# A two-layer hybrid backbone on one core: the expert stage's order on TensorE regrouped, and nine buffers for expert weights

## The chip, the core and the metric

The program runs on one core of a Trainium2 chip. The metric is the device time of one execution, in microseconds (us). The kernel before took 1310.83 us (median of 3 runs, 1310.83 to 1314.21).

A core has engines that run on their own and wait for each other by semaphores: TensorE (PE in the profile; PEld are its weight loads), VectorE (DVE), ScalarE (ACT), GpSimd (POOL) and SyncE (SP), which here issues nearly all DMAs. SBUF is the memory on the core, PSUM the banks that TensorE writes.

## The reference, cut to what matters

Two groups of 128 tokens (prompt and sample) go through two layers, D = 1024, with one set of weights. A layer is a token mixer and a mixture of experts:

```python
mod = silu(c) @ w_mod[l] + b_mod[l]                     # six vectors of 1024: shift, scale, gate, twice
y = token_mixing(x * (1 + scale1) + shift1, ...)        # one input projection, three branches, output projection
x = layer_norm(ALPHA * x + gate1 * y, g, b)
h = x * (1 + scale2) + shift2
gate = top2_of_4_inside_the_best_of_4_groups(h @ w_rg, h @ w_re)       # 16 weights a token, two of them not zero
hid = silu(h @ w_e1[e]) * (h @ w_e3[e])                 # for each of 16 experts: 1024 -> 512
y = sum over e of (hid * gate[e]) @ w_e2[e]             # 512 -> 1024
x = layer_norm(ALPHA * x + gate2 * y, g, b)
```

All weights are float32. An expert has three matrices of 2 MiB: "up 0" (w_e1), "up 1" (w_e3) and "down" (w_e2). The modulation is 12 matrices of 2 MiB a layer.

## The kernel before, in words

Both groups are computed together: 256 tokens. A layer has four stages on TensorE: 18 chunks of the input projection, three branch products, the output projection with the routing, and the experts. Work is written out by hand for each engine, and each engine runs its list in order; `l` is the layer.

**The projection.** A chunk of w_in (2 MiB) comes into one of three ring buffers; the rounds of the branches (`h_round`, `t_round`) stand between the quarters of the chunks at places that `plan` works out. Among the chunks, by `MODS_AFTER`, stand products with a modulation matrix (`mod_products`, L967), 12 in layer 0 and 3 in layer 1. These 2 MiB matrices go through the same ring. All modulation rows must be there at `TURN_AT`, where they are summed and stored; the two gate vectors are read back for the norms.

**The routing.** After the output projection TensorE turns x, makes the routing logits and ranks the tokens of each expert. In layer 0 two more modulation products of layer 1 stand there (`router_mod`, `ROUTER_MODS`), in layer 1 products that are thrown away (`hold_clock`).

**The experts.** The tokens of an expert, at most 64, are gathered by products with a choice matrix (`gather_split`, bfloat16 in three parts, 24 matmuls for half of the features), into `xgT`, for two experts at a time. `up(j, e, i)` is the product of up matrix j with expert e + i: 16 matmuls of shape 128 rows by 64 columns, two beside each other. `down` has the same shape. `hid` is turned by two transposes (128 by 128), the choice matrix too (`sel_turned`), and the result of `down`, weighted on VectorE and split into three bfloat16 parts by ScalarE and VectorE in turn, is spread back to the tokens (`spread_group`, 64 rows by 128 columns, adding up in PSUM). A loop runs over pairs of experts, written out in `pair`; the first and the last pair are apart.

**The loads.** Eight buffers hold expert weights: two for an even expert's up matrices (`ahead_slot`), one for its down matrix (`even_down`), the ring of three for odd experts, and two that are filled once, before the experts begin, with the last expert's up 1 and down (`last_up`, `last_down`). A buffer's next load is issued by SP when `slot_used` says that TensorE has read it (`used_e`), in the order of SP's list (`expert_slot`, `even_slot`, `even_down_slot`). The loads share one DMA queue. The first pair also splits the 256 tokens into three bfloat16 parts on VectorE and ScalarE (`split_tokens`, `middle`), which `gather_split` needs.

At the end of layer 0's experts three modulation matrices (`LAYER_MODS`) come into the freed buffers and their products (L967) stand before layer 1's first chunk.

## Time and profile before

| | us |
|---|---|
| median of 3 runs | 1310.83 |
| profiled execution | 1309.18 |
| its span in the trace | 1307.4 |
| PE busy | 1264.1 (97%) |
| DVE / ACT / POOL busy | 629.6 / 267.2 / 139.2 |
| experts, layer 0 (first up product to last spread) | 442.1 to 667.3 |
| experts, layer 1 | 1070.1 to 1294.6 |

The profiled execution's own time lies 1.8 us over its span. A busy PE counts modelled ends of matmuls, so 97% does not say that nothing is lost; what is lost is read from the starts. In a row of PE a float32 matmul of the program is counted twice, since it is two instructions. In a row of the timeline what stands in square brackets is the idle time before it and what ended it.

### The profile page before, as it was taken

The numbers are of one execution on the slowest core, as the hardware profiler recorded it, in microseconds if no ns is written. First come the engines' busy times: TensorE is split into PE (matmuls) and PEld (weight loads), VectorE is DVE, ScalarE is ACT, GpSimd is POOL, SyncE is SP. The second block draws the span as 40 slices with busy tenths as digits, with TensorE's granted clock in tenths as the row PEclk, the third lists the DMA queues.
The fourth block names the chain that finished last, engine by engine and source line by source line (L and its number), as shares of the span: only waits on it lengthen the run. The fifth ranks groups of instructions, "written<-read, shape, count | busy, mean of one in ns | idle before, by whom it ended". The sixth has DMA issues, their size and how long they took to land.

```text
span 1307.4 us, 18971 instructions
## 1 busy us (share of the span) xinstructions
PE 1264.1 (97%) x7484; PEld 775.6 (59%) x7484; DVE 629.6 (48%) x1217; ACT 267.2 (20%) x572; POOL 139.2 (11%) x115
## 2 busy tenths in 40 slices
PE   6999999999999999999999999999999999999995
PEld 3675577477744655555548656855884465555552
DVE  1225455476333764454452345556753366544444
ACT  0021221233301211111120212203430122111111
POOL 0003432022200000000000034301230000000000
PEclk9999999999999999999999999999999999999998
DMA  9954653756649999999993536254445599999991
GB/s 377 342 228 174 233 210 137 272 227 269 233 160 375 396 427 428 429 429 428 429 403 130 223 131 226 98 199 154 153 155 227 207 348 428 427 428 428 429 428 59
DMA packets 47096, 375.30 MB, mean 287 GB/s; under 512 B 15272, under 2 KB 19512, under 8 KB 23864
## 3 DMA queue, kind: packets, MB, share of 16 engines
q1 hardware_dynamic: 38544, 371.14, 70.5%
q10 hardware_dynamic: 8488, 3.29, 1.0%
q8 instruction: 43, 0.70, 0.2%
q14 instruction: 21, 0.17, 0.0%
HBM read 370.07 MB, written 4.33 MB: 286 GB/s over the span
## 4 chain that ended last, share of the span: by engine, by line
PE 86%; DMA 7%; DVE 5%; issue 1%; ACT 1%; DVEq 0%; SPq 0%; ACTq 0%
PE psum L1275 17%; PE psum L1419 13%; PE psum L1222 9%; PE psum L1269 9%; PE psum L1479 7%; PE psum L1300 6%; PE psum L1314 4%; DMA ring<-in_stream 4%; PE psum L967 3%; PE psum L1427 2%; PE psum L1389 2%; PE psum L1030 2%; PE psum L950 2%; DMA ch<-in_stream 1%; DMA tbuf<-in_stream 1%
## 5 line engine op out<-in xcount | busy, mean ns | idle before, releaser
L1275 PE MATMUL psum<-ring,hT 128*128 128x512 f32 x512 | 228.7, 594 | 1.2 <-DVE hT L1908 0.8
L1275 PEld LDWEIGHTS psum<-ring,hT 128*128 128x128 f32 x512 | 93.5, 190 | 103.4 <-issue 101.1
L1269 PE MATMUL psum<-hT,ring 128*128 128x256 f32 x608 | 136.7, 380 | 0.0
L1269 PEld LDWEIGHTS psum<-hT,ring 128*128 128x128 f32 x608 | 113.7, 190 | 17.8 <-issue 3.5
L1419 PE MATMUL psum<-ch,tbuf 128*64 128x256 f32 x1024 | 113.3, 379 | 0.0
L1419 PE MATMUL psum<-ring,tbuf 128*64 128x256 f32 x960 | 106.8, 379 | 2.2 <-DMA ring<-in_stream 2.2
L1419 PEld LDWEIGHTS psum<-ch,tbuf 128*64 128x64 f32 x1024 | 73.4, 137 | 42.9 <-issue 8.0
L1419 PEld LDWEIGHTS psum<-ring,tbuf 128*64 128x64 f32 x960 | 69.6, 137 | 43.5 <-issue 7.0
L1300 PE MATMUL psum<-ring,tbuf 128*128 128x512 f32 x192 | 82.7, 592 | 0.0
L2565 POOL TENSOR_SCALAR ldata<-ldata 128x512 f32<-128x512 f32 x24 | 50.6, 2108 | 221.0 <-ACT ldata L1728 221.0
L2370 DVE TENSOR_SCALAR tbuf<-psum,tbuf 128x512 f32<-128x512 f32 x32 | 24.0, 751 | 103.1 <-PE psum L1479 103.1
L1300 PEld LDWEIGHTS psum<-ring,tbuf 128*128 128x128 f32 x192 | 36.5, 190 | 45.1 <-issue 45.0
L1479 PE MATMUL psum<-ring,tbuf 128*64 128x512 f32 x256 | 58.5, 598 | 0.9 <-ACT tbuf L1814 0.9
L1314 PE MATMUL psum<-ring,hT 128*128 128x512 f32 x128 | 55.8, 594 | 1.4 <-ACT hT L1762 1.4
L2390 DVE RECIPROCAL tbuf<-tbuf 128x256 f32<-128x256 f32 x32 | 56.1, 1753 | 1.1
L402 POOL TENSOR_TENSOR hbuf<-hbuf 128x512 f32<-128x512 f32 x28 | 45.5, 1627 | 93.4 <-PE psum L1030 93.4
L1222 PE MATMUL psum<-hbuf 128*128 128x256 f32 x240 | 54.9, 381 | 0.1
L1479 PE MATMUL psum<-ch,tbuf 128*64 128x512 f32 x224 | 51.2, 598 | 0.2 <-DMA ch<-in_stream 0.2
L2180 DVE TENSOR_TENSOR ch<-psum,bias_ring 128x512 f32<-128x512 f32 x28 | 19.3, 691 | 63.6 <-PE psum L1275 63.6
L1824 ACT ACTIVATE hbuf<-tbuf 128x512 bf16<-128x512 f32 x30 | 18.9, 630 | 148.2 <-DVE tbuf L2370 148.2
L1222 PEld LDWEIGHTS psum<-hbuf 128*128 128x128 f32 x240 | 44.5, 190 | 7.0 <-issue 1.2
L1427 PE MATMUL psum<-hbuf,tbuf 64*128 64x512 bf16 x360 | 46.8, 379 | 0.0
(349 smaller groups left out, 1607.1 us busy)
## 6 DMA issues: line engine op xcount, KB each, us to landing
ring<-in_stream SPq DMA_DIRECT2D x104, 2048.0 KB, 11.2
ch<-in_stream SPq DMA_DIRECT2D x51, 2048.0 KB, 18.3
bias_ring<-in_b_in SPq DMA_DIRECT2D x26, 256.0 KB, 8.1
ring<-in_stream SPq DMA_DIRECT2D x6, 1024.0 KB, 16.2
ldata<-in_ldata SPq DMA_DIRECT2D x2, 2329.0 KB, 17.5
tbuf<-in_stream SPq DMA_DIRECT2D x2, 2048.0 KB, 14.3
hbuf<-in_ln SPq DMA_DIRECT2D x4, 1024.0 KB, 10.0
ldata<-in_stream SPq DMA_DIRECT2D x2, 2048.0 KB, 12.5
```

The lines of the kernel that those rows point to most:

```text
L402: return engine.tensor_tensor(v, v, other.unsqueeze(3).to_broadcast([P, 2, W // (2 * half), half]), ALU.mult)
L967: mm = pe.matmul(psum[MROWS * j:MROWS * (j + 1), b, :], scZ[:, k, ZC - 2 * m:ZC - 2 * m + MROWS], w[:, k, :], start=(start and k < 4), sto ...
L1222: mm = pe.matmul(psum[:, product_bank(c, p), 0:HALF], a_block(a)[:, k, :], b_block(l, c, b)[:, k, :], start=(k == 0 and not on_top), stop= ...
L1269: mm = pe.matmul(psum[:, b, part * G * P:(part + 1) * G * P], w[:, k, (2 * g + part) * P:(2 * g + part + 1) * P], hT[:, k, :], start=(k == ...
L1275: mm = pe.matmul(bank(PJ + g), hT[:, k, g * P:(g + 1) * P], w[:, k, :], start=(k == 0), stop=(k == KT - 1))
L1300: mm = pe.matmul(bank(BR_BANK[g] + hf), rows_k, w[:, k, hf * W:(hf + 1) * W], start=(k == 0), stop=(k == BT - 1))
L1314: mm = pe.matmul(bank(2 * hf + g), hT[:, k, g * P:(g + 1) * P], w[:, k, :], start=(k == 0), stop=(k == KT - 1))
L1419: mm = pe.matmul(psum[halves_of[hf], UP[j], 0:FE // 2], xgT[:, k, halves_of[i]], w_k[:, hf * (FE // 2):(hf + 1) * (FE // 2)], start=(k == ...
L1427: mm = pe.matmul(bank(Y_MOE[g][hf]), e_selT[i][g][halves_of[hf], :], e_parts[halves_of[hf], s, :], start=opens and s == 0, stop=False)
L1479: mm = pe.matmul(psum[halves_of[hf], OUT, :], ehidT[:, (k % 2) * P + (k // 2) * CAP:(k % 2) * P + (k // 2) * CAP + CAP], w_down[:, k, hf * ...
L2390: mlink(dve.reciprocal(esig, esig))
L2565: pool.tensor_scalar(sig, sig, 1.0, LN_MAX, ALU.add, ALU.min).then_inc(sig_plus, 1)
```

## The change: what it does

1. **Nine buffers.** `extra` (two halves) is a ninth buffer. The buffers that are filled once now hold expert 1's down and up 1 (`second_down`, `second_up`), and `extra` holds expert 1's up 0 first and expert 15's up 0 afterwards. The ring therefore starts with expert 3. SP issues half of `extra`, `second_down` and half of `second_up` (4 MiB) after the loads of the branch matrices; before, the last expert's 4 MiB stood behind the first experts' loads. The norm's and gates' vectors of the second sub-layer (2 MiB) now go where `second_down` lies, and are loaded after expert 1's down product.
2. **Modulations moved.** Layer 1's products with matrices 10 and 11 leave the projection (chunks 6 and 10) and stand in layer 1's routing in place of `hold_clock`. Their rows are summed by one more product, which waits for VectorE's `add_router_mods` and stands before the gather; ScalarE copies the sum out and stores it.
3. **TensorE's order in a pair.** Products of one tile shape stand together, and the spreads of both experts stand in one piece. VectorE's and ScalarE's lists are reordered to match. The turned `hid` and the second half of the gathered tokens get other places in PSUM.
4. The layer's data (`ldata`) is loaded in two pieces; the first 2 MiB come later, since the norm's vectors lie there.

The numbers of lines in this diff are those of the two files; "..." is what is left out.

```diff
-              dict(zip([2, 6, 10], [(1, m) for m in range(9, N_MOD)]))]
-ROUTER_MODS, LAYER_MODS = [4, 5], [6, 7, 8]
+              {2: (1, 9)}]
+ROUTER_MODS, LAYER_MODS = [[4, 5], [10, 11]], [6, 7, 8]
...
+        extra = [hbuf[:, 0:4 * W], spare[:, :, :].rearrange("p a n -> p (a n)")]
+        gathered_late = psum[:, 0:2, FE // 2:FE]
+        hid_out = psum[:, XG, 0:FE // 2]
...
-                        norm_and_gates(l, 0)
+                        norm(l, 0)
+                        gates(l, 0)
+                        sp.wait_ge(t_dve, l * NT + NT)
+                        second = l * SLOTS + FIRST_EXPERT_SLOT + 3
+                        sp.dma_start(extra[1], dram["stream"][second, :, SLOT // 2:]).then_inc(extra_loaded, 16)
+                        sp.dma_start(second_down, dram["stream"][second + 2]).then_inc(second_down_loaded, 16)
+                        sp.wait_ge(proj_read, proj(l, N_IN - 1, 1))
...
-                expert_slot(1, 0, used(l, FIRST_EXPERT[l] - 3))
-                expert_slot(1, 1, used(l, FIRST_EXPERT[l] - 2))
+                expert_slot(3, 0, used(l, FIRST_EXPERT[l] - 3))
+                expert_slot(3, 1, used(l, FIRST_EXPERT[l] - 2))
                 expert_slot(0, 2, used(l, FIRST_EXPERT[l] - 1))
...
                 def first_pass():
...
+                    even_slot(2, 0, used_e(l, 0, 0, 0))
+                    even_slot(2, 1, used_e(l, 0, 0, 1))
+                    expert_slot(3, 2, used_e(l, 0, 0, 2))
                     sp.wait_ge(h2_split, l * G + G)
+                    even_down_slot(2, used_e(l, 0, 0, 2))
+                    sp.wait_ge(slot_used, used_e(l, 0, 1, 0))
+                    for i, piece in enumerate(extra):
+                        sp.dma_start(piece, dram["stream"][l * SLOTS + FIRST_EXPERT_SLOT + 3 * (NE - 1), :, ...])
+                    sp.wait_ge(slot_used, used_e(l, 0, 1, 2))
+                    norm(l, 1)
+                    gates(l, 1)
...
+                    def next_pair(e, last=False):
+                        even_slot(e + 2, 0, used_e(l, e, 0, 0))
+                        even_slot(e + 2, 1, used_e(l, e, 0, 1))
+                        if not last:
+                            expert_slot(e + 3, 0, used_e(l, e, 1, 0))
+                        expert_slot(e + 3, 1, used_e(l, e, 1, 1))
+                        even_down_slot(e + 2, used_e(l, e, 0, 2))
+                        expert_slot(e + 3, 2, used_e(l, e, 1, 2))
...
+                if l + 1 == DEPTH:
+                    pe.wait_ge(h2_ready, l * 4 + 4)
+                    pe.wait_ge(rows_added, len(MOD_ADDS))
+                    pe.matmul(psum[0:MROWS, EX + 1, :], fold, rows[:, l, :], start=True, stop=True).then_inc(rows_summed, 1)
...
                 def pair(e, first=False, last=False):
...
+                    n = step(l, e)
+                    up(1, e, 0, ahead=True)
+                    pe.wait_ge(moe_chain, n * 3 + 3)
+                    up(0, e, 1, first=first, last=last)
+                    turn_hidden(n)
+                    turn_choice(n)
+                    up(1, e, 1, first=first)
+                    down(n, e, 0, first, last)
+                    if not last:
+                        gather_split(n + 2, 0, first=first)
+                        pe.wait_ge(hid_ready, n + 2)
+                        gather_split(n + 2, 1)
+                        pe.wait_ge(xg_ready, n + 3)
+                    turn_hidden(n + 1)
+                    turn_choice(n + 1)
+                    if not first:
+                        spread_rows(n - 1, 1)
+                    if last:
+                        down(n + 1, e, 1, first, last)
+                        spread_rows(n, 0)
...
+                    else:
+                        spread_rows(n, 0, opens=first)
+                        pe.wait_ge(xg_ready, n + 4)
+                        pe.wait_ge(hidT_ready, n + 2)
+                        up(0, e + 2, 0, ahead=True)
+                        down(n + 1, e, 1, first, last)
```

TensorE, the loop over pairs (layer 0), before. L1419 is `up` (32 matmuls are two of them), L1479 `down`, L1389 a half of the gather, L1447 the turned choice, L1458 the turned `hid`, L1427 the spreads (6 are half an expert's).

```order
L1447 MATMUL psum<-tbuf 128x132 x2
L1427 MATMUL psum<-hbuf,tbuf 128x512 x6
L1458 MATMUL psum<-const,tbuf 128x128 x2
L1427 MATMUL psum<-hbuf,tbuf 128x512 x6
L1479 MATMUL psum<-ch,tbuf 64x512 x8
...
L1419 MATMUL psum<-ring,tbuf 64x256 x32
...
L1389 MATMUL psum<-tbuf,hbuf 128x128 x24
L1447 MATMUL psum<-tbuf 128x132 x2
L1427 MATMUL psum<-hbuf,tbuf 128x512 x12
L1458 MATMUL psum<-const,tbuf 128x128 x2
...
L1389 MATMUL psum<-tbuf,hbuf 128x128 x24
...
L1479 MATMUL psum<-ring,tbuf 64x512 x8
```

The same loop now. L1438 is `up`, L1495 `down`, L1401 the gather, L1468 the turned choice, L1460 the turned `hid`, L1446 the spreads.

```order
L1438 MATMUL psum<-ring,tbuf 64x256 x16
...
L1460 MATMUL psum<-const,tbuf 128x128 x2
L1468 MATMUL psum<-tbuf 128x132 x2
...
L1438 MATMUL psum<-ring,tbuf 64x256 x16
L1495 MATMUL psum<-ch,tbuf 64x512 x8
...
L1401 MATMUL psum<-tbuf,hbuf 128x128 x48
...
L1460 MATMUL psum<-const,tbuf 128x128 x2
L1468 MATMUL psum<-tbuf 128x132 x2
L1446 MATMUL psum<-hbuf,tbuf 128x512 x24
...
L1438 MATMUL psum<-ch,tbuf 64x256 x16
...
L1495 MATMUL psum<-ring,tbuf 64x512 x8
```

The number of matmuls of a pair is the same; the shape changed nine times in a round of the loop before and changes five times now.

SP, from the second sub-layer's first expert loads to the loop (layer 0), before: `ch` is `ahead_slot` and `even_down`, `ldata`, `hT`, `values` and `bias_ring` hold the last expert, `hbuf` and `spare` the norm's and gates' vectors.

```order
L853 DMA ring<-in_stream 128x4096 x3
L865 DMA ldata<-in_stream 128x4096
L871 DMA hT<-in_stream 128x2048
L871 DMA values<-in_stream 128x1024
L871 DMA bias_ring<-in_stream 128x1024
L759 DMA hbuf<-in_ln 128x2048
L761 DMA spare<-row_mem 128x2048
L858 DMA ch<-in_stream 128x4096 x2
L853 DMA ring<-in_stream 128x4096 x3
L880 DMA ch<-in_stream 128x4096
L853 DMA ring<-in_stream 128x4096
```

The same place now: the ring holds expert 0's down and expert 3, and `hbuf` with `spare` is the ninth buffer.

```order
L872 DMA ring<-in_stream 128x4096 x3
L883 DMA hbuf<-in_stream 128x2048
L885 DMA hT<-in_stream 128x2048
L877 DMA ch<-in_stream 128x4096 x2
L872 DMA ring<-in_stream 128x4096
L890 DMA ch<-in_stream 128x4096
L900 DMA hbuf<-in_stream 128x2048
L900 DMA spare<-in_stream 128x2048
L764 DMA ldata<-in_ln 128x2048
L770 DMA ldata<-row_mem 128x2048
```

The last expert's 4 MiB are gone from the front, one ring load stands between the first even loads and the even down matrix, where three stood, and the vectors stand last, behind expert 1's down product.

VectorE, the first pair, before: L2341 and L2344 split the tokens, L2389 to L2391 are the silu of expert 1, L2366 and L2370 weight expert 0's rows, L2384 takes gathered tokens in.

```order
L2351 TENSOR_SCALAR tbuf<-const,tbuf 128x64 x4
L2341 TENSOR_TENSOR hbuf<-ch,hbuf 128x1024
L2344 TENSOR_TENSOR hbuf<-hbuf 128x1024
L2341 TENSOR_TENSOR hbuf<-ch,hbuf 128x1024
L2344 TENSOR_TENSOR hbuf<-hbuf 128x1024
L2366 TENSOR_REDUCE tbuf<-tbuf 128x1
L2370 TENSOR_SCALAR tbuf<-psum,tbuf 128x512
L2376 TENSOR_TENSOR tbuf<-tbuf,hbuf 128x512
L2379 TENSOR_TENSOR hbuf<-tbuf,hbuf 128x512
L2389 TENSOR_SCALAR tbuf<-tbuf 128x256
L2390 RECIPROCAL tbuf<-tbuf 128x256
L2391 TENSOR_TENSOR tbuf<-tbuf,psum 128x256
```

The same place now: L2396 and L2399 split, L2449 to L2451 are the silu, L2457 makes expert 1's `hid`, L2421 and L2426 weight expert 0's rows, L2444 takes tokens in.

```order
L2396 TENSOR_TENSOR hbuf<-ch,hbuf 128x1024
L2399 TENSOR_TENSOR hbuf<-hbuf 128x1024
L2449 TENSOR_SCALAR tbuf<-tbuf 128x256
L2450 RECIPROCAL tbuf<-tbuf 128x256
L2451 TENSOR_TENSOR tbuf<-tbuf,psum 128x256
...
L2457 TENSOR_TENSOR tbuf<-tbuf,psum 128x256
L2421 TENSOR_REDUCE tbuf<-tbuf 128x1
L2426 TENSOR_SCALAR tbuf<-psum,tbuf 128x512
L2444 COPY tbuf<-psum 128x512
L2431 TENSOR_TENSOR tbuf<-tbuf,hbuf 128x512
L2444 COPY tbuf<-psum 128x512
L2437 TENSOR_TENSOR hbuf<-tbuf,hbuf 128x512
```

Expert 1's silu and `hid` now stand between the split of the tokens and the weighting of expert 0's rows, and the two copies of gathered tokens stand inside the split of the rows.

## Rows read from the trace of the kernel before

**Rows 1.** The page's first part: busy us, share of the span, instructions.

```profile
PE 1264.1 (97%) x7484; PEld 775.6 (59%) x7484; DVE 629.6 (48%) x1217; ACT 267.2 (20%) x572; POOL 139.2 (11%) x115
```

**Rows 2.** Stretches: length, busy of each engine, clock granted, DMA share, GB/s.

```profile
438.40:442.10 3.70, 3.70 (x32) 3.60 (x32) 1.01 (x2) 0.33 (x1) 0.00 (x0) 1.00 0.98 363
442.10:667.30 225.20, 220.82 (x1873) 123.16 (x1873) 112.46 (x242) 39.40 (x80) 0.00 (x0) 1.00 1.01 427
...
672.70:1056.00 383.30, 381.14 (x1642) 250.86 (x1642) 184.15 (x317) 87.53 (x193) 69.26 (x56) 1.00 0.50 184
1064.80:1070.06 5.26, 5.26 (x32) 5.14 (x32) 0.69 (x1) 0.34 (x1) 0.00 (x0) 0.69 1.00 356
1070.06:1294.60 224.54, 220.76 (x1869) 121.96 (x1868) 112.77 (x242) 39.39 (x80) 0.00 (x0) 1.00 0.92 390
```

**Rows 3.** PE in order of time, a pair: start, length, line, tiles, shape, count.

```profile
522.81 3.65 PE L1479 MATMUL psum<-ring,tbuf 128*64 128x512 f32 x16
...
534.27 0.44 PE L1458 MATMUL psum<-const,tbuf 128*128 128x128 f32 x2
534.64 0.82 PE L1427 MATMUL psum<-hbuf,tbuf 64*128 64x512 bf16 x6
...
538.88 7.08 PE L1419 MATMUL psum<-ring,tbuf 128*64 128x256 f32 x64
545.89 1.51 PE L1389 MATMUL psum<-tbuf,hbuf 128*128 128x128 bf16 x24
547.24 0.28 PE L1447 MATMUL psum<-tbuf 128*128 128x132 bf16 x2
...
548.85 0.44 PE L1458 MATMUL psum<-const,tbuf 128*128 128x128 f32 x2
549.12 1.50 PE L1389 MATMUL psum<-tbuf,hbuf 128*128 128x128 bf16 x24
550.55 0.65 PE L1479 MATMUL psum<-ring,tbuf 128*64 128x512 f32 x2
```

**Rows 4.** PE in order of time, expert 13's up 0.

```profile
626.92 3.67 PE L1419 MATMUL psum<-ring,tbuf 128*64 128x256 f32 x32 [1.18 <-DMA ring<-in_stream]
```

**Rows 5.** Ring loads, issue to landing: issued at 946.2; seven, issued 570.5 to 625.8.

```profile
DMA to landing us min/median/max: 7.6/7.6/7.6
...
DMA to landing us min/median/max: 20.3/23.6/25.6
```

**Rows 6.** SP in order of time: expert 2's up matrices, layer 0.

```profile
445.84 3.78 SPq L858 DMA_DIRECT2D ch<-in_stream  x2
```

**Rows 7.** DVE in order of time, the first pair of layer 0.

```profile
448.99 0.42 DVE L2391 TENSOR_TENSOR tbuf<-tbuf,psum 128x256 f32<-128x256 f32 x1
...
450.90 1.22 DVE L2341 TENSOR_TENSOR hbuf<-ch,hbuf 128x1024 f32<-128x1024 f32 x1
453.31 1.23 DVE L2344 TENSOR_TENSOR hbuf<-hbuf 128x1024 bf16<-128x1024 f32 x1 [1.19 <-ACT hbuf L1798]
...
458.39 0.75 DVE L2370 TENSOR_SCALAR tbuf<-psum,tbuf 128x512 f32<-128x512 f32 x1
459.83 0.69 DVE L2376 TENSOR_TENSOR tbuf<-tbuf,hbuf 128x512 f32<-128x512 f32 x1 [0.70 <-ACT hbuf L1824]
```

**Rows 8.** PE in order of time: from layer 0's experts to layer 1.

```profile
667.27 5.36 PE L967 MATMUL psum<-ch,scZ 128*32 128x512 f32 x48
```

**Rows 9.** PE in order of time, layer 1, the modulation product after chunk 6.

```profile
788.23 1.92 PE L967 MATMUL psum<-ring,scZ 128*32 128x512 f32 x16
790.09 1.09 PE L950 MATMUL psum<-const,hbuf 128*128 128x128 f32 x8
```

**Rows 10.** In order of time: a sum of rows, the router's add, layer 1's gather.

```profile
335.76 1.05 PE L1249 MATMUL psum<-rows,const 128*32 128x512 f32 x2
...
438.04 0.68 DVE L2335 TENSOR_TENSOR rows<-rows,psum 128x512 f32<-128x512 f32 x1
...
1064.79 5.34 PE L1399 MATMUL psum<-tbuf,ch 128*128 128x128 f32 x32 [0.90 <-DVE tbuf L2351]
```

More of the change, by code:

```diff
@@ new lines, in turn_hidden, with turn_choice @@
+                def turn_hidden(n):
+                    pe.wait_ge(hid_ready, n + 1)
+                    for j in range(2):
+                        mm = pe.transpose(hid_out[:, j * P:(j + 1) * P], ehid[:, j * P:(j + 1) * P], ident)
+                    mm.then_inc(hid_turned, 1)
+                def turn_choice(n):
+                    pe.wait_ge(sel_ready, n + 1)
+                    pe.wait_ge(out_read, n)
+                    for g in (1, 0):
+                        mm = pe.matmul(psum[:, OUT, (1 - g) * (P + 4):(2 - g) * (P + 4)], e_sel[:, g, :], around_ident[:, 4 * g:4 * g + P + 4],
+                                       start=True, stop=True)
+                    mm.then_inc(sel_turned, 1)
@@ new lines, in spread_rows, with down @@
+                def spread_rows(n, i, opens=False):
+                    pe.wait_ge(selT_ready, n + 1)
+                    pe.wait_ge(eout_ready, n + 1)
+                    for g in range(G):
+                        spread_group(i, g, opens)
+                def down(n, e, i, first, last):
+                    pe.wait_ge(hidT_ready, n + 1)
+                    pe.wait_ge(selT_ready, n + 1)
+                    from_even = i == 0 and not first
+                    if from_even:
+                        pe.wait_ge(even_down_loaded, e * 8 + l * ((NE // 2 - 1) * 16))
+                    elif i == 0:
+                        pe.wait_ge(slot_loaded[ring_e(l, 2)], first_down_arrived(l))
+                    elif first:
+                        pe.wait_ge(second_down_loaded, l * 16 + 16)
+                    else:
+                        pe.wait_ge(slot_loaded[ring_e(l, 2)], arrived_e(l, e + i, 2))
+                    w_down = w_down_even if from_even else w_down_second if i == 1 and first else w_down_ring
+                    for k in range(BT):
+                        for hf in range(2):
+                            mm = pe.matmul(psum[halves_of[hf], OUT, :], ehidT[:, (k % 2) * P + (k // 2) * CAP:(k % 2) * P + (k // 2) * CAP + CAP],
+                                           w_down[:, k, hf * W:(hf + 1) * W], start=(k == 0), stop=(k == BT - 1))
+                    mm.then_inc(slot_used, 1)
@@ new lines, in pair @@
+                def pair(e, first=False, last=False):
+                    n = step(l, e)
+                    sigmoid_exp(n + 1, e, 1)
+                    hidden(n)
+                    choice(n, turned_slots[0], first)
+                    if first:
+                        middle(0)
+                        middle(1)
+                    split_rows(n, 0)
+                    hidden(n + 1)
+                    choice(n + 1, turned_last if last else turned_slots[1], first)
+                    if last:
+                        act.wait_ge(eout_ready, n + 1)
+                        act.sem_inc(out_high, 1)
+                        act.sem_inc(out_middle, 1)
+                    else:
+                        sigmoid_exp(n + 2, e + 2, 0)
+                        if first and l + 1 == DEPTH:
+                            act.wait_ge(rows_stored, (l + 2) * 16)
+                        split_rows(n + 1, 1)
@@ new lines, in pair @@
+                    n = step(l, e)
+                    hidden(n, e, 0)
+                    if not last:
+                        pick_pair(n + 2, e + 2, e_pick_b)
+                    if first:
+                        for g in range(G):
+                            split_tokens(g)
+                    silu(n + 1)
+                    select(n + 1, e + 1)
+                    hidden(n + 1, e, 1)
+                    weighted_rows(n, e, 0, turned_slots[0], first)
+                    if not last:
+                        tokens_in(n + 2, 0, XG)
@@ new lines, in pair @@
+                    left_of_high(n, 0)
+                    if not last:
+                        tokens_in(n + 3, 1, None)
+                    left_of_middle(n, 0)
+                    if not last:
+                        select(n + 2, e + 2)
+                        if first:
+                            for g in range(G):
+                                link(ts(x[:, g, :], x[:, g, :], ALPHA, None, ALU.mult))
+                        silu(n + 2)
+                        weighted_rows(n + 1, e, 1, turned_slots[1], first)
+                        left_of_high(n + 1, 1)
+                        left_of_middle(n + 1, 1)
+                    else:
+                        weighted_rows(n + 1, e, 1, turned_last)
+                        dve.sem_inc(out_left, 1)
+                        dve.sem_inc(eout_ready, 1)
```

329 lines of the change are left out of this document (121 added, 208 removed).

## The prediction

> **What bounds the kernel now.** I read the page's first part, then the stretches, then TensorE's order of time in the experts, then the loads. The first says that TensorE is busy for 97% of the span [rows 1], so a gain must take work or waits from it. The stretches say that the two expert stages take 225.2 and 224.5 us and that in layer 0's the DMA queue has no free time at all, 427 GB/s with a share of 1.01 [rows 2]. Both are near their limit there, so I looked at which is nearer. A pair of experts takes 550.55 - 522.81 = 27.74 us on TensorE [rows 3]. A matrix of 2 MiB (2.097 MB) takes 2.097 / 427 = 4.91 us, and a pair needs six: 29.5 us. The loads thus lose 1.7 us a pair against TensorE, and only the lead from before the first pair pays for it. One sees that in the loads: a lone one lands 7.6 us after its issue, near the end of the stage they take 20.3 to 25.6 us [rows 5], and at 626.92 TensorE waits 1.18 us for one [rows 4]. So before, the loads catch up with TensorE just as the stage ends. Whatever makes TensorE faster here is worth something only if the loads come earlier too.
>
> **TensorE's order.** The matmuls of a pair stay. What goes is four of nine changes of shape. Their price: a turn of hid followed by another product of its shape takes 549.12 - 548.85 = 0.27 us, followed by a spread 534.64 - 534.27 = 0.37; half a gather takes 547.24 - 545.89 = 1.35 before its own shape and 550.55 - 549.12 = 1.43 before the other [rows 3]. So 0.1 us each, 0.4 us a pair, and a pair becomes 27.3 us. Two up products take 545.89 - 538.88 = 7.01 us with the change behind them, so 3.43 us for one alone.
>
> The Trainium skill (TensorEngine Tiling (Array Packing), section Key Properties) says that changing the tiling mode drains TensorE, where changing only the tile does not. The trace agrees in direction, with the 0.1 us above. By that rule alone fewer changes are a gain in every pair; what that would come to is the first rival below.
>
> **The loads of the expert stage, layer 0.** The first pair decides, so I carry it with rows of before.
> - Expert 0's silu ends on VectorE at 448.99 + 0.42 = 449.41 [rows 7]. TensorE now needs it for expert 1's up 0, 0.5 us after the second up product (442.1 + 2 x 3.43 = 449.0). Then up 0 (3.43), turns with two changes (0.65), up 1 and down (6.87): expert 0's down ends at 460.4.
> - Expert 2's up matrices are issued as before, at 445.84 and 3.45 us later [rows 6], but the queue is empty by then: the preload ends at about 443.5 (worked out: half of the ninth buffer and of expert 1's up 1, 1 MiB each at 2.45 us, issued when layer 0's routing products are done, about 435.8, with 7.6 - 4.9 = 2.7 us ahead of the first). They land at 458.5. The next load waits for expert 0's down: issued 460.7, flowing from 463.5. So the queue stands empty for some 5 us twice, and some 5 us before the preload's last part. These 15 us eat up what the 4 MiB that now come in the branch stage (2 x 4.91 = 9.8 us) would have gained, and more.
> - The three loads then last to 463.5 + 3 x 4.91 = 478.2. Behind them come the norm's and gates' vectors (4.9 us together), which wait for expert 1's down. When does that end? VectorE now splits the tokens (1.22, a wait of 1.19 for ScalarE, 1.23, twice [rows 7]) before expert 1's silu (2.5 us). ScalarE starts its part only after TensorE's turns, about 454.4, so the split ends at 460.3, silu and hid at 463.75, and TensorE waits 1.9 us before the second half of the gather (that half overwrites a bank which hid is read from). Weighting, copy, split of the rows, 0.75 and 0.69 each with 0.70 for ScalarE [rows 7], make the spread ready at 467.6: another 2.0 us of waits. Up and down (6.87) end at 475.9; the vectors flow from 478.9, 0.7 us after the queue ran dry, to 483.8.
> - From there the queue is full: 29 matrices to expert 12's down, 483.8 + 29 x 4.91 = 626.2. TensorE's own pace would bring it there at 475.9 + 5 x 27.3 + 11.2 = 623.6, so it waits 2.6 us in all and the shorter pairs are swallowed.
> - Rest of the stage by TensorE: down 3.43, gather and turns 3.3, spreads 2.7, a wait of 0.35 for expert 14's up 0, then 30.2 us (up, down, two ups, turns, up and down, turns, spread 1.4, down 3.7, spread 1.3, last spread 1.9). It ends at 666.2, against 667.27 [rows 8].
> - Layer 1's three modulation matrices are the next in the queue; the last lands at 626.2 + 9 x 4.91 = 670.4. Its product began at 667.27 + 2 x 5.36 / 3 = 670.85 before [rows 8]. Gain at the start of layer 1: **0.4 us** (bounds 1.2 and a loss of 1).
>
> The Trainium skill (DMA: Bandwidth & Descriptors, section Where 436 GB/s comes from) says that for HBM to SBUF the HBM side binds at about 358 GB/s. By that a matrix would take 5.86 us, and 33 of them 31 us more in each layer than I count. The trace disagrees: 427 GB/s over 225 us [rows 2]. I keep 427.
>
> **The moved modulations.** A product with its change of shape costs 790.09 - 788.23 = 1.86 us [rows 9], and two leave layer 1's projection. TensorE is busy there 381.14 of 383.30 us [rows 2], so nothing else is late when they go: **3.7 us** (bounds 0, if a branch round is late instead, and 3.7). Their loads leave as well, hidden before. In the routing they stand in for products that are thrown away, as in layer 0: nothing (bounds -0.5 and 0.5), since their 4 MiB start at about 1021 less the gain, more than 25 us ahead. What layer 1 gets anew is the sum of rows: the gather waits for the router's add, which ended at 438.04 + 0.68 = 438.7 in layer 0, 0.3 us after the gather began at 438.4 [rows 2, 10], plus some 0.3 to be seen by TensorE, and for the sum itself, 1.05 us [rows 10]. In place of 1064.79 the gather begins 1.6 us later. Before, TensorE's clock fell to its lower level there, 1.2 GHz (granted 0.69 in the mean over 5.26 us, against 3.70 us of the same work in layer 0) after waits of which 0.90 us is the last [rows 2, 10]. With the sum inside, the gap before it grows, so I let the clock fall as before: **1.6 us lost** (bounds 0, if the clock stays, as in layer 0, and 3.2, if it falls twice).
>
> **The expert stage, layer 1.** The same course as in layer 0, 666.2 - 442.1 = 224.1 us, against 224.54 [rows 2]: **0.45 us** (bounds 2.5, PE's pace alone, and a loss of 3). ScalarE's late copy of the sum and the store have the length of a pair to hide in. The final norms stay.
>
> **The sum.** 0.4 + 3.7 - 1.6 + 0.45 = 2.95 us less. The profiled execution took 1309.18 (its span is 1307.4); it becomes 1306.2. The median of the runs is 1.65 above it: 1310.83 - 2.95 = **1307.9**, 0.22% less. What a measurement of this kernel can tell from no change is about 0.3%, 3.9 us, so the likeliest outcome lies just within it.
>
> **Rivals.**
> - *TensorE sets the end of both expert stages* (by what the page on tiling says, fewer drains are a gain). For it: TensorE waits for loads just once, 1.18 us [rows 4]. Against: the queue's rate has no reserve. Six pairs by 0.4, that wait, the weighting at the end (about 0.9, now beside a spread), less 2.6 in the first pair (4.4 us of waits against about 1.8): 1.9 to 2.3 a layer, so 2.1 x 2 in place of 0.85: 1304.6. If the first pair's waits don't come either, 1300.
> - *The clock falls in the first pair* (slower). TensorE stands still twice there, 1.9 and 2.0 us, longer than the 0.90 us before the fall in layer 1. One fall costs 5.26 - 3.70 = 1.56 us [rows 2] and delays expert 1's down, hence the vectors, hence the full queue, by as much; two a layer cost 6.2: 1314.1. From one fall a layer on the change is no longer faster. Against it: in layer 0 the waits before the gather brought no fall.
> - *The projection doesn't get shorter*, since a round of the branches takes the place of the products: 1307.9 + 3.7 = 1311.6. Against: the 2 us of waits in 383.
>
> **Chances.** The forecast 0.53, its own range 1304.5 to 1311; TensorE sets the end 0.18; clock 0.15; projection 0.09; something else 0.05, mostly slower. Below 1306.9 lie a bit over 0.4 of the forecast and nearly all of the first rival: 0.40. Above 1314.8 lie half of the clock rival and what else is slower: 0.12. Within: 0.48. Range 1301.5 to 1315.
>
> **What would show it.** Right: in the expert stages of after, loads 4.9 us apart without a gap from about 464 to 670, gaps of some 5 us twice between 443 and 464, waits of TensorE for DMA from expert 10 on, 2 to 3 us in all; pairs of 27.3 us in the middle and over 29 at the end; waits of 1.5 to 2 us at the gather's second half and before the first spread; two modulation products fewer. Wrong: pairs of 27.3 us to the end, or a granted clock of 0.5 in the first pair, or a wait of some 2 us where the products were.

## The result, and the profile after

The changed kernel takes 1313.79 us (median of 20 runs, 1310.87 to 1318.03) against 1310.82 before (20 runs): a ratio of 1.0021, 95% interval 1.0013 to 1.0030. It is slower by about 2.8 us, where 2.9 us faster was forecast; the time lies inside the range. The profiled execution took 1313.28, its span is 1311.5. Where its 4.1 us went is read from the stretches (columns as in [rows 2]): layer 0's experts to the end of the last spread, layer 1's projection, its routing from the ranking to the first up product, its experts; the last row is the middle of layer 0's experts.

```profile
443.39:670.57 227.18, 218.36 (x1870) 124.16 (x1869) 112.56 (x242) 36.75 (x80) 0.00 (x0) 1.00 0.97 407
675.97:1055.35 379.38, 377.21 (x1622) 249.88 (x1622) 182.79 (x315) 87.58 (x193) 68.88 (x56) 1.00 0.53 201
1061.89:1070.90 9.01, 7.63 (x44) 6.60 (x44) 2.65 (x11) 2.91 (x4) 0.00 (x0) 0.81 0.66 242
1070.90:1298.75 227.85, 219.72 (x1869) 124.00 (x1868) 112.36 (x242) 36.75 (x80) 0.00 (x0) 0.99 0.90 378
480.00:629.00 149.00, 145.50 (x1276) 84.17 (x1271) 71.55 (x154) 23.63 (x54) 0.00 (x0) 1.00 1.01 428
```

| stretch | before | after | forecast | measured |
|---|---|---|---|---|
| experts, layer 0, with the boundary | 225.17 | 227.18 | -0.4 | +2.0 |
| projection, layer 1 | 383.46 | 379.38 | -3.7 | -4.1 |
| routing, layer 1 | 7.45 | 9.01 | +1.6 | +1.6 |
| experts, layer 1 | 224.55 | 227.85 | -0.45 | +3.3 |

They sum to 2.8 us. (That the medians differ by 2.8 us too is in part chance: these are two executions, each somewhere among the runs of its kernel.) The other 1.3 us is the start. TensorE's second modulation product took 3.30 us in place of 1.92, first the kernel before, then the changed one; in the trace's records the clock came to its upper level at 13.30 us and at 18.04:

```profile
15.33 1.92 PE L967 MATMUL psum<-tbuf,scZ 128*32 128x512 f32 x16 [1.93 <-DMA tbuf<-in_stream]
...
15.21 3.30 PE L981 MATMUL psum<-tbuf,scZ 128*32 128x512 f32 x16 [2.12 <-DMA tbuf<-in_stream]
```

The first ranking of layer 0 began anywhere from 436.1 to 440.1 in the kernels below, and in the kernel before at 436.20 in one trace and at about 437.6 in that of e4, which starts with the same list. So I do not put that to the change; all the stage times below leave it out.

TensorE in layer 0's first pair (columns as in [rows 3]), then a pair from the middle by its first and last up product:

```profile
450.74 1.95 PE L1438 MATMUL psum<-hbuf,tbuf 128*64 128x256 f32 x16 [0.22 <-DVE tbuf L2451]
...
461.86 1.51 PE L1401 MATMUL psum<-tbuf,hbuf 128*128 128x128 bf16 x24
464.92 1.51 PE L1401 MATMUL psum<-tbuf,hbuf 128*128 128x128 bf16 x24 [1.54 <-DVE tbuf L2457]
...
468.71 1.47 PE L1446 MATMUL psum<-hbuf,tbuf 64*128 64x512 bf16 x12 [1.79 <-DVE hbuf L2437]
...
504.36 3.62 PE L1438 MATMUL psum<-ch,tbuf 128*64 128x256 f32 x32
...
531.68 3.62 PE L1438 MATMUL psum<-ch,tbuf 128*64 128x256 f32 x32
```

The forecast waits of the first pair are there (0.22, 1.54 and 1.79 for 0.5, 1.9 and 2.0), and a pair takes 531.68 - 504.36 = 27.32 us for 27.74 [rows 3]. In the last pair there are two waits that the forecast does not have; ScalarE's rows (ACT) stand among TensorE's:

```profile
656.70 3.60 PE L1495 MATMUL psum<-ch,tbuf 128*64 128x512 f32 x16
660.23 0.44 PE L1460 MATMUL psum<-const,tbuf 128*128 128x128 f32 x2
...
661.19 0.63 ACT L1857 ACTIVATE hbuf<-tbuf 128x512 bf16<-128x512 f32 x1 [7.34 <-DVE tbuf L2426]
661.31 0.28 PE L1468 MATMUL psum<-tbuf 128*128 128x132 bf16 x2 [0.64 <-DVE tbuf L2426]
661.51 1.47 PE L1446 MATMUL psum<-hbuf,tbuf 64*128 64x512 bf16 x12
...
662.58 0.63 ACT L1859 ACTIVATE hbuf<-tbuf 128x512 bf16<-128x512 f32 x1 [0.76 <-DVE tbuf L2431]
663.12 0.37 ACT L1845 ACTIVATE tbuf<-psum 128x256 f32<-128x256 f32 x1
...
663.86 3.65 PE L1495 MATMUL psum<-ring,tbuf 128*64 128x512 f32 x16 [0.88 <-ACT tbuf L1845]
```

The first wait, 0.64 us, is for VectorE. The turned choice is written over what expert 14's down product left, so VectorE's weighting of those rows (L2426) has to read that first; in the other pairs the gather stands between the two and covers it, in the last pair there is no gather. The second, 0.88 us, comes of ScalarE's order. Expert 15's turned hid is there at 660.7, but ScalarE copies it (L1845) only at 663.12, behind its two parts of expert 14's split (L1857, L1859). Nothing is left for TensorE in that time: the spreads that stood between these steps before now stand in one piece.

The queue's gaps in the first pair:

```profile
443.70:448.30 4.60, 4.60 (x46) 3.08 (x44) 3.94 (x23) 0.38 (x1) 0.00 (x0) 1.00 0.23 48
458.50:462.60 4.10, 4.10 (x29) 1.60 (x26) 2.87 (x4) 1.06 (x1) 0.00 (x0) 1.00 0.04 16
478.50:480.00 1.50, 1.50 (x18) 1.00 (x14) 0.69 (x1) 0.74 (x2) 0.00 (x0) 1.00 0.76 208
```

The loads on both sides of the last of them, by their issue (start, length of the issuing) and their time from issue to landing:

```profile
463.29 0.69 SPq L900 DMA_DIRECT2D spare<-in_stream  x1
477.63 0.43 SPq L770 DMA_DIRECT2D ldata<-row_mem  x1
...
spare<-in_stream SPq DMA_DIRECT2D x1, 1024.0 KB, 16.9
ldata<-row_mem SPq DMA_DIRECT2D x1, 1024.0 KB, 9.4
```

TensorE's waits for loads in layer 0's experts (total us, times, longest), two rows of the kernel before and then three of the changed one:

```profile
PE psum L1419 <- DMA ring<-in_stream: 1.2, 1, 1.2
PE psum L1479 <- DMA ch<-in_stream: 0.2, 1, 0.2
...
PE psum L1495 <- DMA ch<-in_stream: 2.8, 3, 1.3
...
PE psum L1438 <- DMA ch<-in_stream: 0.6, 3, 0.2
PE psum L1438 <- DMA ring<-in_stream: 0.4, 2, 0.2
```

The queue stands nearly empty for 4.6 and 4.1 us, moves half its rate (208 GB/s) for 1.5 us, and from then on it is full (428 GB/s). TensorE waits 3.8 us for loads, against 1.4 us before.

Last, the clock in layer 1's first pair:

```profile
1096.65:1100.06 3.41, 3.41 (x18) 1.50 (x16) 1.19 (x2) 0.00 (x0) 0.00 (x0) 0.50 1.03 442
```

It is the lower level, 1.2 GHz, right behind the two waits. Layer 0's first pair kept the upper one in this execution.

### The profile page after: what moved, and what is told of

Read it like the earlier page. It is cut to its first block, busy times and chain, and to the rows that moved or that the text cites. A ratio compares the mean times of both kernels' runs of the same rounds, so it can differ in the third digit from the quotient of the medians.

```text
span 1311.5 us, 19020 instructions
## 1 busy us (share of the span) xinstructions
PE 1259.3 (96%) x7478; PEld 777.8 (59%) x7478; DVE 628.2 (48%) x1216; ACT 262.6 (20%) x573; POOL 138.8 (11%) x115
## 4 chain that ended last, share of the span: by engine, by line
PE 82%; DMA 9%; DVE 6%; issue 2%; ACT 1%; SPq 0%; ACTq 0%; DVEq 0%
PE psum L1291 17%; PE psum L1438 12%; PE psum L1236 9%; PE psum L1285 9%; DMA ch<-in_stream 8%; PE psum L1316 6%; PE psum L1495 6%; PE psum L1330 4%; PE psum L981 3%; PE psum L1044 2%; PE psum L1446 2%; PE psum L964 2%; PE psum L1401 1%; DMA tbuf<-in_stream 1%; PE psum L1412 1%
## 5 line engine op out<-in xcount | busy, mean ns | idle before, releaser
L1438 PE MATMUL psum<-ch,tbuf 128*64 128x256 f32 x1024 | 117.1, 382 | 1.2 <-DMA ch<-in_stream 1.2
L1438 PEld LDWEIGHTS psum<-ch,tbuf 128*64 128x64 f32 x1024 | 72.4, 138 | 49.2 <-issue 12.4
L1438 PE MATMUL psum<-ring,tbuf 128*64 128x256 f32 x832 | 94.9, 381 | 0.5 <-DMA ring<-in_stream 0.5
L1438 PEld LDWEIGHTS psum<-ring,tbuf 128*64 128x64 f32 x832 | 58.4, 137 | 30.3 <-DMA ring<-in_stream 1.1
L2449 DVE TENSOR_SCALAR tbuf<-tbuf 128x256 f32<-128x256 f32 x32 | 9.4, 293 | 111.8 <-ACT tbuf L1840 111.8
L1495 PE MATMUL psum<-ring,tbuf 128*64 128x512 f32 x256 | 57.7, 593 | 1.8 <-ACT tbuf L1845 1.8
L1495 PE MATMUL psum<-ch,tbuf 128*64 128x512 f32 x224 | 50.7, 594 | 5.1 <-DMA ch<-in_stream 5.1
L1857 ACT ACTIVATE hbuf<-tbuf 128x512 bf16<-128x512 f32 x30 | 18.9, 630 | 176.0 <-DVE tbuf L2426 176.0
L2426 DVE TENSOR_SCALAR tbuf<-psum,tbuf 128x512 f32<-128x512 f32 x32 | 24.0, 751 | 60.6 <-PE psum L1495 47.5
```

Source lines behind the costliest of these rows:

```text
L1438: mm = pe.matmul(psum[halves_of[hf], UP[j], 0:FE // 2], xgT[:, k, halves_of[i]], w_up[k][:, hf * (FE // 2):(hf + 1) * (FE // 2)], start=(k ...
L1495: mm = pe.matmul(psum[halves_of[hf], OUT, :], ehidT[:, (k % 2) * P + (k // 2) * CAP:(k % 2) * P + (k // 2) * CAP + CAP], w_down[:, k, hf * ...
```

## The experiments

Each is timed against runs of the kernel before on its own chip; the ratio is to those. Kernels whose stages take the same time differ by up to 0.0018 in it, some 2.4 us (the changed kernel 1.0021, e6 1.0003), so the argument goes by the stages; there, two traces of one and the same list differ by up to some 0.55 us (e5 below). Stage times run from the first up product to the begin of the last spread, in the changed kernel and those built on it with the spread's weight load: 223.23 us in layer 0 and 222.56 in layer 1 before, 225.15 and 225.75 in the changed kernel. The 225.75 holds the fall of the clock; e1, e2, e5 and e7 have none there, so what they gain in layer 0 is the cleaner figure. "Layer 1's way" is from that last spread of layer 0 to layer 1's ranking: 397.25 before, 393.35 after.

**e1: the tokens' split earlier.** ScalarE's list in the first pair:

```diff
+                    if first:
+                        middle(0); middle(1)
                     sigmoid_exp(n + 1, e, 1)
                     hidden(n)
                     choice(n, turned_slots[0], first)
-                    if first:
-                        middle(0); middle(1)
```

> Theory (the loads bind the stage, and the first pair's waits delay them): ScalarE makes its part of the token split before the exponential of expert 1, so VectorE's split ends about 3 us earlier; the waits of 1.54 us before the gather's second half and 1.79 us before the first spread shrink to under 0.8 together in each layer. Expert 1's down product ends some 2.7 us earlier, the norm's and gates' vectors are issued 2.7 us earlier and every later load lands 2.7 us earlier. TensorE's waits for loads stay near 1.7 us a layer, each expert stage gets 2.7 us shorter, and the clock does not fall in layer 1's first pair (another 1.6 us): the median falls by 5 to 7 us, to 1307 to 1309. Rival (the first pair's waits are hidden, since the loads are late anyway): the waits for loads grow by what the first pair gains, and the time changes by less than 1.5 us.

Measured: 1309.75, ratio 0.9990 (0.9979 to 1.0002).

```profile
442.01:666.24 224.23, 216.23 (x1859) 123.39 (x1860) 112.01 (x241) 36.67 (x80) 0.00 (x0) 1.00 0.97 407
...
1059.58:1066.96 7.38, 6.00 (x44) 4.98 (x44) 2.64 (x11) 2.92 (x4) 0.00 (x0) 1.00 0.78 295
1066.96:1291.42 224.46, 216.30 (x1859) 122.77 (x1860) 111.73 (x241) 36.66 (x80) 0.00 (x0) 1.00 0.91 383
```

```profile
PE psum L1495 <- DMA ch<-in_stream: 3.9, 3, 1.3
PE psum L1446 <- DVE hbuf L2437: 1.2, 1, 1.2
```

The first pair's waits fell from 3.3 to 1.2 us, but layer 0's stage only by 0.9, since the waits for loads grew by 1.1. In layer 0's stage the rival was right on the size. By the ratios the whole kernel gained 4.1 us over the changed one, more than the rival allowed: the clock stayed up in layer 1, in the routing too, which is 1.6 us shorter and which neither expected.

**e2: the vectors last.** `norm(l, 1)` and `gates(l, 1)` move behind `next_pair(NE - 4, last=True)` in SP's list.

> The norm's and gates' vectors (2 MiB) are loaded behind the last expert's matrices, not between expert 1's down and expert 4. Theory (the queue binds): all loads from expert 4's up to expert 15's land 4.9 us earlier, TensorE's waits for loads (1.7 us a layer) vanish; layer 0 gains 1.3 us only, since the three modulation matrices at its end still land at the same time (the last at 673), layer 1 gains 1.6: about -3 us, 1311. Rival (buffers that come free late set the landings, not the queue): landings and waits stay as they are, within 0.5 us. Rival 2: the norm now waits for its vectors, and the time grows by 2 us or more.

Measured: 1312.27, ratio 1.0015 (0.9998 to 1.0032). Layer 0's last products:

```profile
663.57 1.88 PE L1452 MATMUL psum<-tbuf 64*128 64x512 f32 x8
665.38 1.92 PE L980 MATMUL psum<-ch,scZ 128*32 128x512 f32 x16
669.06 1.92 PE L980 MATMUL psum<-ch,scZ 128*32 128x512 f32 x16 [1.76 <-DMA ch<-in_stream]
673.98 1.92 PE L980 MATMUL psum<-ch,scZ 128*32 128x512 f32 x16 [2.99 <-DMA ch<-in_stream]
```

The stages became 221.19 and 221.33, 4.0 and 4.4 us shorter, and layer 0's waits for loads went from 3.8 to 0.5 us: they were the queue's, twice what I had expected (I had counted only the 1.7 us around expert 12's down, and those around expert 10's cost as much). In layer 0 it comes back as 1.76 + 2.99 us in front of layer 1's modulations, which end the same queue. By the ratios the time is only 0.8 us under the changed kernel's, where the theory had 3. The profiled execution, 1308.45, was the fastest of the twelve and has no fall of the clock in a first pair; the mean granted clock of the twelve, 0.9918, is the lowest of all kernels here. So the clock is the likely reason, but no run shows it.

**e3: the modulations back.** The table has `{2, 6, 10}` again, the routing of layer 1 its `hold_clock`, and no sum of rows stands before the gather.

> The two modulation products go back into layer 1's projection, and the routing of layer 1 gets its thrown-away products back; the rest is as in the changed kernel. Theory: the projection costs 4.0 us more, the routing 1.6 us less, so +2.4 us, 1316.2; if the fall of the clock in layer 1's first pair goes with the sum of rows, +0.9. Rival (the moved modulations are what made the kernel slower, by the sum of rows and the clock): the time falls by 1.5 us or more. Rival 2: moving them was worth nothing, within 1 us.

Measured: 1317.21, ratio 1.0046 (1.0028 to 1.0064), by the ratios 3.3 us over the changed kernel. Layer 1's way is 397.76 (4.4 more), the routing 7.56 (1.5 less). So the move is worth some 2.9 us, and it is not what made the kernel slower.

**e4: the kernel before, with the vectors last.** The same edit in before.py's list, asking what loads cost there.

> The kernel before, with the norm's and gates' vectors loaded behind the last expert's matrices. It asks what the loads cost there. Theory (before, the loads catch up only at the very end): all loads of the experts land 2.0 us earlier, the one wait for a load goes, so layer 0's experts take 1.2 us less and layer 1's 1.0 less, while the modulations behind layer 0 come 2.9 us later and their last product waits 0.6: -1.6 us in all. Rival (the loads bind that kernel as they bind the changed one): 3 to 4 us less in each expert stage.

Measured: 1309.75, ratio 0.9983 (0.9972 to 0.9995). Stages 222.46 and 222.33: 0.8 and 0.2 less, where the changed kernel gave 4.0 and 4.4. But the edit did not free that kernel of its loads. It brought them only some 0.8 us earlier by the stage's own time, and a wait of 0.7 us stayed where 1.2 had been:

```profile
627.51 3.67 PE L1419 MATMUL psum<-ring,tbuf 128*64 128x256 f32 x32 [0.66 <-DMA ring<-in_stream]
```

So the run bears out little; that the loads cost little before is read from their waits, 1.4 us in all.

**e5: the last pair.**

```diff
                     turn_hidden(n + 1)
+                    if last:
+                        spread_rows(n - 1, 1)
                     turn_choice(n + 1)
...                  # ScalarE, last pair: hidden(n + 1), choice(n + 1), then split_rows(n, 0)
```

> In the last pair the spread of expert 13 goes ahead of the turned choice, and ScalarE copies expert 15's turned hid and choice before it splits expert 14's rows. Theory: the waits of 0.64 and 0.88 us in the last pair of each layer shrink to about 0.5 together, 1.0 us a layer, -2 us, 1311.8; layer 0's gain is real only as long as the modulation matrices at its end land in time (the last at 673, needed at 673.1 then). Rival (the waits only move): the spread of expert 14 waits instead for its rows, and the time changes by less than 0.5 us.

Measured: 1311.13, ratio 1.0002 (0.9989 to 1.0016), and

```profile
656.10 3.60 PE L1495 MATMUL psum<-ch,tbuf 128*64 128x512 f32 x16
...
660.00 1.47 PE L1446 MATMUL psum<-hbuf,tbuf 64*128 64x512 bf16 x12
661.40 0.29 PE L1468 MATMUL psum<-tbuf 128*128 128x132 bf16 x2
662.22 3.65 PE L1495 MATMUL psum<-ring,tbuf 128*64 128x512 f32 x16 [0.53 <-issue]
```

Stages 223.55 and 224.22, 1.6 and 1.5 us shorter. Not all of that is the edit. From expert 14's down to expert 15's it is 662.22 - 656.10 = 6.12 us here and 663.86 - 656.70 = 7.16 in the changed kernel: about 1.05 of the 1.52 us came back, and 0.53 stays as the time that the turned hid takes to come back from ScalarE. What the edit took out came back whole, since it stands behind the last load that is waited for. The other 0.55 us of layer 0 lies ahead of the last pair, where both lists are the same and the loads landed earlier in this trace; in layer 1 the fall of the clock is missing.

**e6: expert 15's up 0 first.** SP issues the two halves of `extra` right behind expert 2's up matrices.

> Expert 15's up 0 is issued ahead of the loads that wait for expert 0's down (as soon as expert 1's up 0 is read), so it fills the queue where it stood empty for some 4 us. Theory (the queue is filled, but the vectors behind expert 1's down set its next start): the loads of the first pair land 4.3 us earlier, the queue then runs dry until the vectors come as before, and everything from the vectors on lands where it did; the time stays within 0.7 us of the changed kernel's 1313.8. Rival (every load moves up by what is filled): all landings 4.3 us earlier, the waits for loads (3.8 us in layer 0's experts) go, 2 to 4 us less a layer, 1306 to 1310.

Measured: 1312.25, ratio 1.0003 (0.9990 to 1.0016). The queue, filled and then dry:

```profile
463.00:474.00 11.00, 7.66 (x68) 4.47 (x67) 7.01 (x17) 1.81 (x4) 0.00 (x0) 0.84 0.98 390
474.00:480.50 6.50, 6.50 (x48) 3.13 (x46) 3.41 (x6) 1.01 (x2) 0.00 (x0) 1.00 0.19 63
```

The gap moved by one place, as the theory had it: the vectors wait for expert 1's down. Stages 225.67 and 225.73, no shorter. The granted 0.84 of the first row holds a fall of the clock behind the first pair's second wait, in layer 0 this time; layer 1 has one too, as in the changed kernel, so there the two are like for like. By the ratio the kernel is 2.4 us under the changed one, which no stage shows.

**e7: both (e6 and e1).**

> The last edit and the earlier split together. Theory (the two gate each other): the vectors are issued some 2 us earlier, as with the earlier split alone, and now find the queue empty, so the loads from expert 4 on land 2 to 3 us earlier in their stage than in the changed kernel (1.0 with the split alone), each expert stage gets 2 to 3 us shorter than the changed kernel's 225.15 and 225.75 (0.9 and 1.3 with the split alone), and the mean granted clock stays at the 0.995 of the split alone: 1305 to 1308. Rival (what the split alone gave is all there is): stages of 224.2 and 224.5, 1309.7.

Measured: 1307.36, ratio 0.9971 (0.9960 to 0.9983). Stages 222.24 and 222.22, 2.9 and 3.5 us shorter, where e1 alone gave 0.9 and 1.3 and e6 nothing. Each removes the wait that hid the other. (Layer 1's figures hold the missing fall as well.)

**e8: all five.** e1, e2, e5, e6, and in layer 1 `add_router_mods` stands ahead of VectorE's wait for the ranks.

> The five edits together: earlier split, expert 15's up 0 first, vectors last, the last pair's order, and layer 1's rows added before the ranks come, so that their sum stands in the wait before the gather. Theory: no load is waited for in the experts (4.0 us a layer gained with the vectors last), the last pair gives 1.0 to 1.6, the split 2.9, less what TensorE's own pace then bounds: expert stages of 217 to 220 us against 225.15 and 225.75, no lateness of layer 1's modulations (393.3 from the last spread to layer 1's ranking, not 398), layer 1's route 7.6 in place of 9.0: 1296 to 1301. Rival (the loads of layer 0 still end at the same time, and the modulations wait): layer 0 gains nothing, 1302 to 1306.

Measured: 1303.68, ratio 0.9939 (0.9920 to 0.9958). Stages 218.50 and 218.25, the routing 6.01 for 9.01; but layer 1's way is 399.95, 6.6 us longer, with 2.43 and 2.98 us of waits before the modulations and a fall of the clock right behind them:

```profile
669.05 1.92 PE L980 MATMUL psum<-ch,scZ 128*32 128x512 f32 x16 [2.43 <-DMA ch<-in_stream]
673.95 2.67 PE L980 MATMUL psum<-ch,scZ 128*32 128x512 f32 x16 [2.98 <-DMA ch<-in_stream]
```

The rival took back layer 0's gain.

**e10: products that are thrown away in the waits.** `hold_clock(1, bank(2))` before `pe.wait_ge(hid_ready, n + 2)` and before the first spread.

> The changed kernel with two products that are thrown away, one in each wait of the first pair (before the gather's second half and before the first spread). Theory (the falls of the clock that the changed kernel shows more often come from TensorE standing still there): stages as in the changed kernel within 0.3 us where the clock holds, mean granted clock over the runs 0.995 in place of 0.993, the median 1.5 us less, 1312.3. Rival (the falls have nothing to do with these waits): clock 0.993, 1313.8.

Measured: 1311.74, ratio 1.0006 (0.9994 to 1.0018), mean granted clock 0.9943, standard error 0.0006, from 0.9932 with 0.0006. Its trace has no fall in either first pair, and 0.64 and 0.88 us of the waits are left; but the difference in the mean is not clear, and the trace, the slowest execution of the twelve (1317.46), has a fall in layer 0's gather ahead of the first pair. Open by this run.

**e11: the five, the vectors in layer 0 behind expert 4's first up matrix.**

> The five edits, but in layer 0 the vectors go behind expert 4's first up matrix, where the queue still stood empty for 3.1 us, and stay last in layer 1. Theory (layer 0 ends by the queue): the experts' loads land 1.8 us later than with the five edits, the modulations 3.1 us earlier; layer 0's experts 219 to 220.5 us in place of 218.5, from the last spread to layer 1's ranking 394 to 396 in place of 399.95: 1299.5 to 1301.5. Rival (the later loads cost TensorE as much as the modulations gain): 1303 to 1304.

Measured: 1298.24 (6 executions, as e12), ratio 0.9899 (0.9882 to 0.9917), faster than both kernels and 1.3 us below the low end of what was expected.

```profile
443.42:663.57 220.15, 215.83 (x1860) 123.35 (x1861) 112.06 (x241) 36.79 (x80) 0.00 (x0) 1.00 0.98 414
663.57:1056.90 393.33, 390.78 (x1732) 256.60 (x1728) 192.23 (x341) 91.91 (x203) 68.88 (x56) 1.00 0.54 204
1056.90:1062.92 6.02, 6.02 (x45) 4.98 (x45) 2.61 (x11) 2.91 (x4) 0.00 (x0) 1.00 0.89 329
1062.92:1281.21 218.29, 215.47 (x1860) 123.03 (x1861) 111.87 (x241) 36.78 (x80) 0.00 (x0) 1.00 0.95 395
```

**e12: the five, the vectors last in layer 1 alone.**

> The five edits, but in layer 0 the vectors stay where the changed kernel has them, behind expert 1's down, and go last in layer 1 alone. Theory: layer 0's experts take the 222.24 us of the two edits together less 1.5 for the last pair, 220.7, and the modulations are in time, 393.4; layer 1 as with the five edits: 1299.5 to 1301.5. Rival: as with the five edits, 1303.7, since what the experts lose the modulations gain.

Measured: 1299.09, ratio 0.9905 (0.9887 to 0.9922). Stages 221.17 and 218.21, layer 1's way 393.35. Layer 0 is 0.5 us over the forecast.

**e13: e1 in layer 1 alone.**

> The changed kernel with the earlier split in layer 1 alone. It asks whether the falls of the clock belong to the first pair's waits of their own layer. Theory (a fall comes from TensorE standing still shortly before it): layer 0 and layer 1's routing as in the changed kernel (stage 225.15 us, route 9.0 with a fall to the lower level), no fall in layer 1's first pair, layer 1's stage 224.5; mean granted clock over the runs 0.994, between the 0.9927 of the kernels with both layers' waits and the 0.9952 of those without; 1312 to 1313. Rival (the fall in layer 1's routing goes wherever the split is early, by chance of the traces taken so far or by something later in the program): route 7.4 without a fall, clock 0.995, 1310 to 1311.

Measured: 1312.25, ratio 1.0004 (0.9992 to 1.0016), mean clock 0.9936 (standard error 0.0005). Layer 0's first pair shows a fall right behind its waits, layer 1's none:

```profile
471.25:474.66 3.41, 3.41 (x18) 1.55 (x16) 0.94 (x2) 0.00 (x0) 0.00 (x0) 0.50 1.05 447
```

That is what the theory said of the first pairs. It fails on the routing: 7.39 us without a fall, though nothing ahead of it was changed and its wait of 1.38 us for the rows stayed:

```profile
1066.93 1.02 PE L1384 MATMUL psum<-rows,const 128*32 128x512 f32 x2 [1.38 <-DVE rows L2393]
```

## Why the prediction was wrong

Its direction was wrong by two terms of the expert stages; the rest of the sum held. The times of after are 1.27 us late by the start; that is taken off in this section.

- **TensorE's order: right.** 27.32 us a pair for 27.3. The gain of 0.42 us a pair is there and, as forecast, does not reach the end, since the loads set the pace. The Trainium skill (TensorEngine Tiling (Array Packing), section Key Properties) has the drain at a change of tiling mode; the trace agrees, at 0.1 us each.
- **The first pair: right.** Expert 0's down ended at 460.6 for 460.4, expert 1's at 475.8 for 475.9. e1, e6 and e7 show the chain as the text had it: split, expert 1's down, vectors, full queue.
- **The vectors' load: too small.** "the vectors flow from 478.9, 0.7 us after the queue ran dry, to 483.8": they landed at 485.7. The load ahead of them (`spare`) landed at 463.29 + 16.9 - 1.27 = 478.9 for 478.2, and they took another 6.8 us (to 477.63 + 9.4 - 1.27) where 5.6 were forecast. Both stand right behind an empty place of the queue, in the second case at half its rate (208 GB/s). With 29 matrices behind them, 4.9 us each as forecast, expert 12's down began at 627.8 for 626.2. That is 1.6 us of each layer. Why the queue comes up late is not shown.
- **The step that failed: "Rest of the stage by TensorE".** It gave the last pair 30.2 us and a wait of 0.35 us, 40.0 from expert 12's down to the end; it took 670.57 - 629.05 = 41.5. I added up TensorE's products and did not walk the lists of the engines that answer: with no gather there, the turned choice waits for VectorE's weighting (0.64), and with the spreads in one piece, expert 15's turned hid is queued behind ScalarE's two halves of a split (0.88). That is 1.5 us a layer, and a better order takes out 1.05 of it (e5).
- **The boundary: wrong.** I held that the modulations' loads end at 670.4 and hide TensorE's end at 666.2. TensorE ended at 669.3, and they were in time: the last landed at 671.7, later than forecast too, but its product began only at 672.9. What it costs when TensorE is earlier shows in e2, 1.76 + 2.99 us.
- **The modulations and the routing: right**, 4.1 for 3.7 (the stretch) and 1.6 for 1.6; e3 has 4.4 and 1.5. The "some 0.3" us that the router's add was to take until TensorE sees it was a guess without a row; here the sum begins 0.15 us after the add ends (1064.56 and 1064.41).
- **Layer 1: the same two terms**, 1.6 + 1.5, and a fall of the clock. The two give 224.1 + 3.1 = 227.2; measured 227.85, and the 0.65 left over is about what a fall costs (below).

The rivals. *TensorE sets the end* is refuted: 3.8 us of waits for loads, and 4.0 us less where they come earlier (e2). *The clock falls in the first pair* was real in part. Every fall in a first pair (five, in the traces of the changed kernel, e3, e6 and e13) stood right behind the two waits. Over all executions the mean granted clock was 0.9927 (62 executions, standard error 0.0003) in the kernels with both waits in both layers (the changed one, e2, e3, e5, e6) and 0.9952 (41, 0.0003) in those where the early split left one wait of 1.2 us (e1, e7, e8, e11, e12). But those also lack the fall in layer 1's routing (last section), so that the difference is not the first pair's alone. The kernel before, which has that fall, is the better measure: 0.9946 (92, 0.0002). The difference of 0.0018 (unrounded) of some 1311 us is, with falls of 3.41 us at half the clock, about 1.4 falls more in an execution (an estimate from these rows). What a fall costs is less than the 1.56 us I gave it: layer 0's stage took 225.15 us without one and 225.67 with one (e6, e13), and in e5's trace, without one, it was another 0.55 us shorter ahead of the last pair, so some 0.5 to 1.1 us: part of what TensorE loses it waits less for loads (3.0 us in place of 3.8). So its price was wrong, and the median of 1314.1 that I gave it was met by other causes, by luck. *The projection does not get shorter* is refuted by e3. How much of the 2.8 us the falls make in the mean is not settled; 1.4 falls at that price would be 0.7 to 1.5 us (an estimate), and e10 did not tell.

## What to carry to other kernels

Regrouping one engine's list takes out filler: for each wait that the old order covered, and for each bank that is written again, walk the list of the engine that answers, at the first and the last round of the loop above all. In a queue that is full from some point on, only what starts it earlier or takes bytes out of it counts; look for its empty places and for the wait that opens each, and expect two such waits to hide each other (0.9 and 0, together 2.9 us). A load that can go anywhere belongs where the queue is empty.

## What the runs showed that was not expected

- The clock's fall in layer 1's routing, in the traces of the kernel before, the changed one, e2 to e6 and e10, was missing in all with the early split. In e8, e11 and e12 the wait of 1.38 us ahead of it is gone too (the routing takes 6.0 us), so only e1, e7 and e13 tell, one trace each; in e13 the split that moved comes after it in the program. The routing takes 9.0 us with the fall and 7.39 without. No run here shows why, and chance is not excluded.
- Two empty places of 4.6 and 4.1 us at the head of a queue that then runs at 428 GB/s for 150 us weigh as much as the new order: filling one of them and opening the next load earlier gave 2.9 us in layer 0 (e7), where four changes of shape less in six pairs are 6 x 0.42 = 2.5.
